# ScalarE's order in the pairs behind an up pair, later fetches of the norm weights, and moved norm work, in a two-layer decoder trunk

## The reference

```python
def rmsnorm(x, g):
    y = x32 * lax.rsqrt(jnp.mean(jnp.square(x32), axis=-1, keepdims=True) + RMS_EPS)
    return (y * g).astype(x.dtype)

def sqrelu_mlp(h, w_up, w_down):            # D_MODEL 2048, D_FF 8192
    return jnp.square(jax.nn.relu(h @ w_up)) @ w_down

for layer in range(DEPTH):                  # DEPTH = 2
    h = h + mixer(rmsnorm(h, norm[layer]))  # fox_mixer, then retention_mixer
    h = h + sqrelu_mlp(rmsnorm(h, mlp_norm[layer]), mlp_up[layer], mlp_down[layer])
return rmsnorm(h, final_norm)
```

## Time and profile before

| | before |
|---|---|
| runs, median (lowest to highest) | 2541.56 us (2540.64 to 2543.57) |
| the profiled execution | 2542.16 us, its span 2540.4 us |
| TensorE clock granted, mean | 0.999 of full |
| PE busy | 2501.2 us, 98% |
| VectorE (DVE) busy | 1836.8 us, 72% |
| ScalarE (ACT) busy | 1411.5 us, 56% |
| GpSimd (POOL) busy | 165.3 us, 7% |
| DMA | 534.81 MB, 211 GB/s in the mean |

### The profile page before, as it was taken

How to read it: one execution, slowest core, us unless ns; L and a number is a source line. 1 busy time by engine, 2 the same in 40 slices (tenths; PEclk the granted TensorE clock), 3 DMA queues, 4 the chain that set the end, 5 groups by cost and what they waited for, 6 DMA issues and landing times. The chain is left out here.

```text
span 2540.4 us, 29615 instructions
## 1 busy us (share of the span) xinstructions
PE 2501.2 (98%) x11128; PEld 2045.4 (81%) x11128; DVE 1836.8 (72%) x1941; ACT 1411.5 (56%) x1684; POOL 165.3 (7%) x284
## 2 busy tenths in 40 slices
PE   9999999999999999899999999999999999999998
PEld 8888888787787787778888888888777877878776
DVE  6454556777777777787778867777977777777776
ACT  7454545655555555555556545556555555565554
POOL 0000000000100001111111001101100000000010
PEclk9999999999999999999999999999999999999999
DMA  8454556575847666666665666667666667567584
GB/s 312 149 171 160 166 175 219 189 246 177 264 168 255 208 234 206 221 222 205 216 221 184 234 191 205 204 192 236 222 235 210 226 213 227 208 218 233 188 266 147
DMA packets 210997, 534.81 MB, mean 211 GB/s; under 512 B 17200, under 2 KB 17456, under 8 KB 210480
## 3 DMA queue, kind: packets, MB, share of 16 engines
q1 hardware_dynamic: 192832, 476.65, 55.7%
q0 software_dynamic: 17888, 56.12, 7.2%
q10 hardware_dynamic: 144, 0.26, 0.0%
HBM read 506.74 MB, written 26.21 MB: 210 GB/s over the span
## 5 line engine op out<-in xcount | busy, mean ns | idle before, releaser
L2224 DVE TENSOR_TENSOR w_lo<-work,w_hi 128x1024 fp32r<-128x1024 f32 (+2 forms) x821 | 1074.0, 1327 | 494.6 <-ACT w_hi L1561 491.2
L1561 ACT ACTIVATE w_hi<-work 128x1024 fp32r<-128x1024 f32 (+2 forms) x821 | 917.4, 1137 | 708.6 <-DMA work<-in_w_wide 218.7
L1076 PE MATMUL acc<-w_hi,xT_hi 128*128 128x512 f32 x826 | 325.4, 394 | 4.5 <-DVE xT_lo L2296 2.0
L1078 PE MATMUL acc<-w_hi,xT_lo 128*128 128x512 f32 x826 | 321.9, 390 | 0.0
L1077 PE MATMUL acc<-w_lo,xT_hi 128*128 128x512 f32 x826 | 321.6, 389 | 0.0
L1076 PE MATMUL sc<-w_hi,xT_hi 128*128 128x512 f32 x736 | 287.6, 391 | 0.0
L1078 PE MATMUL sc<-w_hi,xT_lo 128*128 128x512 f32 x736 | 286.6, 389 | 0.0
L1077 PE MATMUL sc<-w_lo,xT_hi 128*128 128x512 f32 x736 | 286.4, 389 | 0.0
L1076 PE MATMUL acc<-w_hi,aT_hi 128*128 128x512 f32 x600 | 237.7, 396 | 8.8 <-DVE aT_lo L2296 4.6
L1078 PE MATMUL acc<-w_hi,aT_lo 128*128 128x512 f32 x600 | 234.2, 390 | 0.0
L1077 PE MATMUL acc<-w_lo,aT_hi 128*128 128x512 f32 x600 | 234.2, 390 | 0.0
(11 more groups left out here) (325 smaller groups left out, 3640.3 us busy)
## 6 DMA issues: line engine op xcount, KB each, us to landing
work<-in_w_stream SPq DMA_DIRECT2D x400, 512.0 KB, 4.6
work<-in_w_wide SPq DMA_DIRECT2D x212, 768.0 KB, 7.5
work<-in_w_wide SPq DMA_DIRECT2D x178, 512.0 KB, 6.7
park<-stage POOLq DMA_DIRECT2D x38, 512.0 KB, 6.1
evac<-park POOLq DMA_DIRECT2D x152, 128.0 KB, 3.7
qk_park<-evac POOLq DMA_DIRECT2D x8, 512.0 KB, 6.4
work<-qk_park POOLq DMA_DIRECT2D x32, 128.0 KB, 5.0
h<-in_x SPq DMA_DIRECT2D x2, 1024.0 KB, 8.7
```

What stands on the lines that cost most here:

```text
L1076: pe.matmul(bank[:, :], x_hi, w_hi[:, c], start=start, stop=False, skip_group_check=True)
L1078: return pe.matmul(bank[:, :], x_lo, w_hi[:, c], start=False, stop=stop, skip_group_check=True)
L1561: ins = act.activation(w_hi[:, ring_cols(place, n)], src[:, first * NB:(first + n) * NB], ACT.Copy)
L2224: ins = dve.tensor_tensor(w_lo[:, c], src[:, first * NB:(first + n) * NB], w_hi[:, c].bitcast(F32), ALU.subtract)
```

## The change

On ScalarE, in a pair behind an up pair: the high parts of W_TAU3 and W_B22 are made ahead of the work on the pair before (W_TAU3 ahead of the relus on e and w, W_B22 between them and `seed_u`), and the second square moves behind `copy_p5`. In pair 1 of mixer 1 (`late_up`) the high part of W_TAU1 goes ahead of the relus on x and z, and on VectorE `turn_blocks` goes behind `tau3`, the low part of W_TAU1 and `tau2`. On VectorE in the norm pairs (i = 0 of mixer 1, i = 15), the add of bank w moves ahead of the low parts of W_TAU3 and W_B22; in pair 15 of mixer 0 the low part of tile 7 moves ahead of the first `gained_after` pair and its `turn_blocks`. GpSimd's queue waits for the low part of pair 15's first tile ahead of two of the fetches of norm weights. And the ring of weight tiles isn't set back to its start at the second mixer, so that the tiles there lie 8 blocks further round.

```diff
         if t == 0 and u in (PAIRS, PAIRS + RET_UNITS):
-            at = 0
+            at = at if at < RING_UNITS_RET else 0
...
             wait_last_use_of_x(mlp_unit(0, PAIRS - 3))
+            pool.wait_ge(mlp_lo, tile_count(mlp_unit(0, PAIRS - 1), W_B11))
             load_gain(1)
...
             wait_last_use_of_x(mlp_unit(1, PAIRS - 3))
+            pool.wait_ge(mlp_lo, tile_count(mlp_unit(1, PAIRS - 1), W_B11))
             load_gain(3)
...
                 if by_pe:
                     square_of_h(1, p_quad, z_out, done)
+                if late_up:
+                    hi(u, W_TAU1)
                 if was_up and not was_plain:
                     relu(0, x_done, acc[0], x_out, done, turn)
                     relu(1, z_done, acc[1], z_out, done, turn)
                     relu_squared(0, x_out, done)
                     relu_squared(1, z_out, done)
-                hi(u, W_TAU1)
+                if not late_up:
+                    hi(u, W_TAU1)
                 hi(u, W_TAU2)
                 if u in LATE:
                     turn_hi(turn - 1, dst, 1)
                 hi(u, W_B21)
                 if was_up:
+                    hi(u, W_TAU3)
                     relu(0, e_done, sc[0], e_out, done, turn + 1)
                     relu(1, w_done, sc[1], w_out, done, turn + 1)
+                    hi(u, W_B22)
...
                 seed_u(u, RET_HEADS * m)
                 if was_up:
                     relu_squared(0, e_out, done)
-                hi(u, W_TAU3)
+                else:
+                    hi(u, W_TAU3)
+                    hi(u, W_B22)
+                copy_p5(u)
                 if was_up:
                     relu_squared(1, w_out, done)
-                hi(u, W_B22)
-                copy_p5(u)
                 seed_z(u)
...
                 lo(u, W_B11)
                 tau1(u)
-                if was_up and not was_plain:
+                if was_up and not was_plain and not late_up:
                     turn_blocks(turn)
                 tau3(u)
                 lo(u, W_TAU1)
                 tau2(u)
+                if late_up:
+                    turn_blocks(turn)
...
                 if was_normed:
                     add_bank(0, p_quad + 1, sc[0], e_done, e_out, done, scaled=not by_pe)
+                    add_bank(1, p_quad + 1, sc[1], w_done, w_out, done, scaled=not by_pe)
                 lo(u, W_TAU3)
                 lo(u, W_B22)
                 if was_up:
                     turn_blocks(turn + 1)
                 seed_e(u)
-                if was_normed:
-                    add_bank(1, p_quad + 1, sc[1], w_done, w_out, done, scaled=not by_pe)
                 lo(u, W_TAU4)
...
                 seed_w(u)
...
+                lo(u, 7)
                 if late_norm and not end:
                     wait_gain(dve, 1)
                     gained_after(0, p_quad, x_out, done)
                     gained_after(1, p_quad, z_out, done)
                     turn_blocks(turn)
-                lo(u, 7)
```

More of the change, by code:

```diff
@@ L1773, in wide_pair @@
                 was_normed = i in (0, PAIRS - 1)
-                late_norm, by_pe = i == PAIRS - 1, i == 0
+                late_norm, by_pe, late_up = i == PAIRS - 1, i == 0, (m, i) == (1, 1)
                 dst = xT_hi if was_normed else aT_hi
```

## The result

The changed kernel takes 2504.24 us in the median (2503.96 to 2505.96), the kernel before 2542.57 beside it (2540.64 to 2550.84): a ratio of 0.9845, 95% interval 0.9822 to 0.9867, 38.3 us less. The profiled execution, the slowest of the four, took 2505.96 us with a span of 2504.2, 36.2 less than that of the kernel before. The prediction was 2501, range 2496 to 2512.

What follows compares the result with a forecast made beforehand. TensorE is busy 98% of the span, so a change pays only where it waits. Terms -31.5 - 4.4 - 4.7 - 1.8 - 0.6 + 0.6 + 1.3 + 0.7 = -40.4 against the median 2541.56 give 2501 us, range 2496 to 2512.

Steps and rivals of the forecast that it cites:

- The ordinary pairs: 15 pairs behind an up pair: all four TensorE waits go, 2.1 us each, -31.5 us.
- near misses: Charge over all pairs for operations that just miss their time, taking it that quarter 3 keeps up: +0.7 us.
- the rival with near misses: Seeds still just miss in the 16 pairs, three misses of 0.1 each: +5 us, 2506; chance 0.11.
- the first rival: Quarter 3's low part stays where it was, seven or eight late pairs wait 1.85 each: +14 us, 2515; chance 0.16.
- Pair 1 of mixer 1: With W_TAU1's high part ahead of the relus, `seed_u` starts as W_B11 is read and waits go: -4.4 us.
- The fetches of norm weights: Moved out of the two pairs 14, their waits there go: -4.7 us in mixer 0, -1.8 in mixer 1.
- The new place: Norm-weight fetches behind pair 15's first low part fall where SP has almost nothing in flight, 0 GB/s from 1060 to 1070.
- Norm work: Earlier add of bank w frees `seed_w`: -0.6 us in the last pair, 0 in pair 0 of mixer 1.
- The norm's chain: Pair 15 of mixer 0 into the retention: first transposition 1.0 us later, chain otherwise fixed, end 0 to 1.0 later: +0.6.
- The wait, "about 4": TensorE's wait at the chain's end, in the retention's first block, grows from 2.0 to about 4 us.
- The clock behind that wait: Half clock behind the wait at the chain's end costs 1.7 us, at three in four: +1.3 us.
- The fourth rest tile: Part of TensorE's waits shifts to this tile, behind the fetch in pair 15 of mixer 0: 1 to 2 us.

Runs made afterwards that it cites:

- ScalarE's order alone: Kernel before with only ScalarE's new order in the 16 pairs behind an up pair (two high parts ahead, second square behind `copy_p5`): 2508.12 us, 0.9866.
- fetches early: Changed kernel without the two new waits of GpSimd's queue, so norm weights are fetched in pair 14 as before: 2506.91 us, 0.9855.
- no `late_up`: Changed kernel with the ordinary order in pair 1 of mixer 1, on both engines: 2509.21 us, 0.9873.
- ring back: Changed kernel with the ring of weight tiles set back to its start at the second mixer, as before: 2505.07 us, 0.9846.
- changed again: The changed kernel, unaltered, measured once more on the chip of the combined kernel: 2503.76 us, 0.9844.
- third turn early: Changed kernel with the third norm quarter's add, product and transposition ahead of the retention's first two low parts and the second quarter's: 2503.01 us, 0.9847.
- chain first: Changed kernel, pair 15 of mixer 0: tile 10's low part ahead of the second transposition, third norm quarter's work behind tile 13's low part: 2506.57 us, 0.9863.
- combined kernel: Changed kernel with tiles 10, 12 and norm products moved into VectorE's idle time, tile 7's low part back behind the first norm products: 2499.61 us, 0.9827.
- tile 7 back: Changed kernel with pair 15 of mixer 0's tile 7 low part again behind the first two norm products and their transposition: 2503.12 us, 0.9846.

## Why the prediction was right, and where it was off

**The ordinary pairs** (-31.5, with +0.7 for near misses): 32.0 us became 1.3, so -30.7, against -30.8. The prediction's times are 4.26 us later than these (625.19 for 620.93). With that taken off, `seed_u`, forecast at 622.56, starts at 622.57, `copy_p5` at 623.85 for 623.85, `seed_z` at 625.21 for 625.21, `seed_w` at 627.97 for 627.93. Two engines' orders laid on the measured clock of the third gave times right to 0.1 us. No wait for `seed_z` or `seed_e` is left in these pairs, so the rival with near misses falls too. Quarter 3 is ready 1.65 to 3.15 us ahead of its first use in the eight late pairs, where before it was 0.35 to 2.87 in six and late in two; the first rival is refuted. Its price was too high as well: it took the 0.35 us of pair 6 for all late pairs. What the prediction did not separate is that the gain is all in the two high parts; the square behind `copy_p5` is worth nothing beside them, and 8 us without them.

**Pair 1 of mixer 1** (-4.4): 4.6 became 0.1, -4.5. Undone alone it costs 5.0 to 5.6, since the new order makes `seed_u` wait 3.7 there instead of 1.8.

**The fetches of norm weights** (-4.7 and -1.8): the losses of the two pairs 14 went as the sum says, 4.7 and 1.9. The step that failed is the cause. ScalarE's order alone takes 4.3 of the 4.7 and 0.4 of the 1.9; what the later fetches add is 0 in mixer 0 and 1.1 in mixer 1 (fetches early against changed). In mixer 0 the order sufficed, and the prediction gave the wait to the fetches; whether they would have sufficed without the order is not shown, since no run has them alone. It did no harm to the sum only because both were made, and that is luck. The new place was misjudged too. The fetches are issued at 1033.52 to 1035.15, some 10 us ahead of pair 15's start, where DMA is busy at 0.60 (1033 to 1036) and 0.53 (1036 to 1040), and not in the stretch with 0 GB/s of the earlier trace rows, which begins at 1040 here. They land 3.5 to 4.3 us after their issue, where it was 6.5 to 8.8 before.

**Norm work.** Last pair -0.6: 0.8 became 0.2. Pair 0 of mixer 1, 0: 3.3 became 3.5. **The norm's chain** (+0.6): its end varies by 1.4 us between four executions of the same instructions (changed, no `late_up`, ring back, changed again: 61.0, 60.0, 60.9, 59.7). With the order of before it came at 59.5, 59.1, 60.2, 60.9 and 60.5 (five kernels), with the changed order at those four and at 61.6 (fetches early), so 0.6 later in the mean; the profiled execution had 1.5, and that the mean meets the forecast is in part chance, with a spread of over 1 us on both sides. The wait, "about 4", was 5.3, and 4.0 to 5.8 in the five.

**The clock behind that wait** (1.7 at three in four, +1.3) is the mis-sized term. It fell every time, and cost 3.0, 1.7, 2.5, 2.4 and 2.2 us, 2.4 in the mean. The 1.7 were taken from one place. The Trainium skill ("TensorE: Matmul & The Clock Gate", Part 1), by which the throttled clock is the default, gave 0.4 more than the sum and was right in direction. With chain and clock together, pair 15 and the block behind it went from 5.7 to 10.1 us, +4.4, where +1.9 was forecast; these 2.5 are most of the 4.2 between -40.4 and -36.2. Of the rest, 0.2 is pair 0, 0.8 lies spread over places outside the steps, and by 0.9 the span shrank less than the summed losses did (37.1); these two are not explained. By the medians of the runs 38.3 were gained, 2.1 less than forecast.

**The fourth rest tile** waits 1.10 us, as forecast, but not behind the fetch: the second transposition stands ahead of tile 10's low part and waits 3.14 us for the park of the first:

```profile
1064.31 1.25 DVE L2298 STREAM_TRANSPOSE stage<-tr 128x1024 f32<-128x1024 f32 x1 [3.14 <-DMA park<-stage]
```

**What holds the chain's end** was not in the prediction, which called the chain fixed. In twelve of the fourteen profiles the low part is done 2.33 to 2.35 us after the last piece of the third quarter's fetch has landed, since ScalarE waits for that piece:

```profile
1102.73 1.06 ACT L1652 ACTIVATE xT_hi<-evac 128x1024 fp32r<-128x1024 f32 x1 [3.34 <-DMA evac<-park]
```

So the 1.4 us between equal kernels are the landing's: 58.7, 57.7, 58.5 and 57.3 us after the pair's start (changed, no `late_up`, ring back, changed again), 1.0 of it in the fetch itself (last section). Why the fetch varies stays open. In the other two, third turn early and chain first, the fetch landed at 55.3 and 50.8, and the end came at 62.2 and 63.1. There the high part of the quarter stands on ScalarE behind high parts of the retention's tiles, and those wait for loads. In chain first:

```profile
1094.37 1.06 ACT L1563 ACTIVATE w_hi<-work 128x1024 fp32r<-128x1024 f32 x1 [4.17 <-DMA work<-in_w_stream]
...
1104.09 1.05 ACT L1652 ACTIVATE xT_hi<-evac 128x1024 fp32r<-128x1024 f32 x1
```

In both kernels low parts were put off for the chain, and SP's loads wait for those: the first load of the retention was issued at 1080.01 and 1082.59, in the changed kernel at 1078.34. The chain moved ahead won its own transfers and lost the loads in front of its last step.

## What to carry to other kernels

Where two edits can each remove the cause of the same wait, price the second with the first already made: a sum of single prices can be right while its reasons are not. Put work ahead on an engine only into time in which that engine waits: low parts moved into VectorE's idle time gained 1 to 2 us, and 4 together with tile 7's old place (with the clock's luck in its profile), while the critical chain moved ahead of low parts gained nothing. Those low parts are also what frees the slots for the next loads, and the chain's last step stands behind the work on these.

## What the hardware did that was not expected

The length of a wait did not decide alone whether the clock falls. A wait of 2.53 us at tile 7 was followed by 1.00 in the kernel before and by 0.86 with ScalarE's order alone; one of 2.42 by 1.00 in the combined kernel and by 0.87 with tile 7 back, with the same instructions up to there. With the third turn early the clock stayed up behind waits of 2.82 and 2.23, while it fell behind 2.92 in the kernel before and behind 2.12 with tile 7 back (0.83 from 1100 to 1110). The prediction's reading, that 2.92 brings the clock down and 2.5 does not, came from one execution and does not hold as a rule. The windows with ScalarE's order alone and with tile 7 back:

```profile
1050.00:1060.00 10.00, 7.24 (x26) 5.30 (x25) 9.91 (x11) 8.27 (x14) 0.54 (x1) 0.86 0.95 330
```

```profile
1050.00:1060.00 10.00, 7.58 (x29) 5.84 (x28) 9.33 (x10) 8.04 (x14) 0.54 (x1) 0.87 1.00 367
```

Even after 3.68 us the fall need not come at once. With ScalarE's order alone the first matmul behind the wait was already slow (0.74, then 0.63, above); with no `late_up` the same wait was followed by matmuls at full pace, and the half clock came 1.6 us later:

```profile
1864.57 0.50 PE L1078 MATMUL mix<-w_hi 128*128 128x512 f32 x1 [3.68 <-ACT mix L1607]
1864.91 0.40 PE L1079 MATMUL mix<-w_lo,w_hi 128*128 128x512 f32 x1
...
1866.14 0.63 PE L1078 MATMUL acc<-w_hi,xT_hi 128*128 128x512 f32 x1
```

All waits of 3.67 us and more, ten in the profiles of after and of the experiments, were followed by half clock, with 1.5 to 3.0 us lost. And the third quarter's fetch through GpSimd's queue took 8.1 to 9.1 us from its issue in four executions of the same instructions, 7.4 in the combined kernel, which alone moves the end of a chain by a microsecond.
